# Two conditioning stages of a four-layer kernel computed inside differential attention, and its output transposes issued later

## The reference

```
silu(c) @ ada_w[i] + ada_b[i]  ->  shift, scale, gate       (layers 0 and 1: 3 x 1024 values, for c and c_ctx)
silu(c) @ w_ada + b_ada        ->  9 x 1024 values           (each of the two later layers, for c_2 and c_ctx_2)
h = rms_norm(x) * (1 + scale) + shift ;   x = x + gate * block(h)
```

```
q, k, v, g = h @ w_in ;  q, k = rope(rms_norm(q)), rope(rms_norm(k))     (keys and values also of the context)
attn = softmax(q1 k1) - lam * softmax(q2 k2) ;  o = attn @ v
y = (rms_norm(o) * silu(g)) @ w_out
```

## Time and profile before

| | |
|---|---|
| median of 3 runs (lowest to highest) | 5384.07 us (5380.6 to 5397.63) |
| the profiled execution's own time, and its span | 5410.06 us, 5408.3 us |
| PE busy | 4611.6 us, 85% of the span |
| PE weight load (beside PE) | 3517.2 us, 65% |
| DVE, ACT, POOL busy | 1674.7, 1243.5, 61.1 us |
| granted TensorE clock, mean | 0.914 |
| DMA | 331.41 MB, mean 61 GB/s |

### The profile page before, as it was taken

One profiled execution on the slowest core, in us unless ns is written; L12 is line 12 of the kernel. 1 busy time (PEld: TensorE's weight loads), 2 busy tenths in 40 slices (PEclk: granted clock), 3 DMA queues, 4 the chain that ended last, 5 costly groups with the idle time before them and its releaser, 6 DMA issues. The chain is left out here.

```text
span 5408.3 us, 86861 instructions
## 1 busy us (share of the span) xinstructions
PE 4611.6 (85%) x39756; PEld 3517.2 (65%) x39756; DVE 1674.7 (31%) x2184; ACT 1243.5 (23%) x1763; POOL 61.1 (1%) x65
## 2 busy tenths in 40 slices
PE   3789999997799975999977688999779997867998
PEld 2466666665466644888854356888658886534786
DVE  1345555552233321322222313222132222042433
ACT  1223333221144421311111203111031121021322
POOL 0000000000000000000002000000000000010000
PEclk7899999998899986999988778999879998978999
DMA  5100000001110018112111001121541211100222
GB/s 221 42 19 19 19 19 19 19 3 48 43 47 32 16 36 305 56 59 71 51 39 48 0 31 63 56 73 54 191 148 61 69 56 43 71 0 32 100 98 74
DMA packets 45308, 331.41 MB, mean 61 GB/s; under 512 B 4401, under 2 KB 8882, under 8 KB 21298
## 3 DMA queue, kind: packets, MB, share of 16 engines
q1 hardware_dynamic: 44978, 326.37, 16.8%
HBM read 324.26 MB, written 2.10 MB: 60 GB/s over the span
## 5 line engine op out<-in xcount | busy, mean ns | idle before, releaser
L617 PE MATMUL banks<-x_hi,w_hi 128*128 128x512 f32 (+1 forms) x2464 | 860.0, 349 | 29.6 <-DVE x_lo L718 29.6
L618 PE MATMUL banks<-x_lo,w_hi 128*128 128x512 f32 (+1 forms) x2464 | 855.7, 347 | 0.0
L619 PE MATMUL banks<-x_hi,w_lo 128*128 128x512 f32 (+1 forms) x2464 | 853.9, 347 | 0.0
L617 PEld LDWEIGHTS banks<-x_hi,w_hi 128*128 128x128 f32 x2464 | 471.0, 191 | 104.7 <-DVE x_lo L718 28.3
L619 PEld LDWEIGHTS banks<-x_hi,w_lo 128*128 128x128 f32 x2464 | 471.5, 191 | 57.4
L618 PEld LDWEIGHTS banks<-x_lo,w_hi 128*128 128x128 f32 x2464 | 472.2, 192 | 54.2
L618 PE MATMUL banks<-g_lo,w_hi 128*128 128x512 f32 (+1 forms) x1232 | 423.9, 344 | 0.0
L617 PE MATMUL banks<-g_hi,w_hi 128*128 128x512 f32 (+1 forms) x1232 | 423.6, 344 | 0.0
L619 PE MATMUL banks<-g_hi,w_lo 128*128 128x512 f32 (+1 forms) x1232 | 423.3, 344 | 0.0
L897 PE MATMUL banks<-x_normed_first,weight_ring_first 128*128 128x256 f32 (+1 forms) x1024 | 370.9, 503 | 3.0 <-ACT small L1219 3.0
L628 ACT CAST w_hi<-landing 128x2048 fp32r<-128x2048 f32 (+1 forms) x152 | 255.7, 1682 | 494.4 <-PE banks L619 494.4
(11 more groups left out here) (366 smaller groups left out, 5789.5 us busy)
## 6 DMA issues: line engine op xcount, KB each, us to landing
landing<-in_w SPq DMA_DIRECT2D x88, 1024.0 KB, 4.8
weight_ring_first<-in_ada_w SPq DMA_DIRECT2D x30, 2048.0 KB, 8.9
landing<-in_w SPq DMA_DIRECT2D x64, 704.0 KB, 4.0
weight_ring_end<-in_ada_w SPq DMA_DIRECT2D x18, 2048.0 KB, 8.8
weight_ring_first<-in_rw_pair SPq DMA_DIRECT2D x8, 2048.0 KB, 8.0
weight_ring_first<-in_da_head SPq DMA_DIRECT2D x8, 2048.0 KB, 7.8
weight_ring_mix<-in_w_in SPq DMA_DIRECT2D x12, 1024.0 KB, 4.8
weight_ring_mix<-in_w_out SPq DMA_DIRECT2D x8, 1024.0 KB, 4.9
```

The source lines that it names most:

```text
L617: nc.tensor.matmul(o, wh, xh[:, k, c0:c0 + cn], start=k == 0, stop=False)
L618: nc.tensor.matmul(o, wh, xl[:, k, c0:c0 + cn], start=False, stop=False)
L619: ins = nc.tensor.matmul(o, wl, xh[:, k, c0:c0 + cn], start=False, stop=k == kt - 1)
```

## The change

The second context load and the two later conditioning stages are gone as stages. Their 36 tiles of weights are loaded, multiplied, copied and transposed inside `diff_attention`, through one buffer of 2 MB in the arena. Four tiles stand in the part before the first scores, and one with each of the 4 x 8 blocks of queries, ahead of `values`; each tile's transpose stands ahead of the next block's `transposes`. The products and their transpose share the last quarter of bank 5. ACT does both copies out of PSUM; DVE adds all biases at once at the end. The values of both later layers have their own columns (48 to 191). The output transposes of head i-1, DVE's `finish` before them and ACT's copy after them now stand in head i, behind its first scores and 8 key products.

```diff
+                def ada_weights(n):
+                    if n:
+                        sp.wait_ge(rows_done.h, rows_done.at(n - 1, 4))
+                    sp.dma_start(ada_w, self.dram[f"ada2_w{n // 18}"][n % 18]).then_inc(ada_ready.h, 16)
...
+                head_weights(0)
+                sp.dma_start(lamv, self.dram["da_lam"]).then_inc(lam_loaded.h, 16)
+                sp.dma_start(rope, self.dram["tables"][:, at:at + n_rope]).then_inc(lam_loaded.h, 16)
+                ada_weights(0)
+                head_weights(1)
+                for n in range(1, EARLY):
+                    ada_weights(n)
+                sp.dma_start(self.x3(self.X)[:, :, LAT:T], self.dram["ctx2_t"]).then_inc(context_loaded.h, 16)
+                for i in range(HEADS):
+                    for q in range(QT):
+                        ada_weights(EARLY + QT * i + q)
+                        if q == 0 and i + 2 < HEADS:
+                            head_weights(i + 2)
...
+                    if i or q:
+                        ada_turn(EARLY + QT * i + q - 1)
                     for t in range(NB):
                         ins = nc.tensor.transpose(bank(4, T)[:, t * P:t * P + P], attn[:, q % 2, t * P:t * P + P], ident)
...
+                    ada_rows(EARLY + QT * i + q)
                     for t in range(NB):
                         ins = mm(bank(5)[:, 256:256 + P], AT[:, q % 2, t], V(i, t), start=t == 0, stop=t == NB - 1)
                     ins.then_inc(pv_done.h, 1)
...
+                def ada_rows(n):
+                    pe.wait_ge(ada_ready.h, ada_ready.at(n, 16))
+                    if n:
+                        pe.wait_ge(cols_taken.h, cols_taken.at(n - 1, 1))
+                    for kt in range(KT):
+                        for g in range(4):
+                            ins = mm(ada_bank[32 * g:32 * g + 32, :], sil[:, kt, :], ada_w[:, kt, g * P:g * P + P], start=kt == 0, stop=kt == KT - 1)
+                            if kt == KT - 1:
+                                ins.then_inc(rows_done.h, 1)
...
+                def ada_turn(n):
+                    pe.wait_ge(rows_copied.h, rows_copied.at(n, 1))
+                    nc.tensor.transpose(ada_bank, rows[:, n % 2], ident).then_inc(turned.h, 1)
...
                 fill = projections(0)
-                pull(fill, 20)
+                pull(fill, 10.2)
+                pe.wait_ge(silu_ready.h, silu_ready.at(0, 1))
+                ada_rows(0)
+                pull(fill, 6.8)
+                ada_turn(0)
+                ada_rows(1)
+                pull(fill, 3)
+                ada_turn(1)
                 pe.wait_ge(rec_ready.h, rec_ready.at(0, 1))
                 pe.wait_ge(lam_ready.h, lam_ready.at(0, 1))
                 broadcast(0, QT, 0)
                 broadcast(2, NB, 8)
+                ada_rows(2)
                 pull(fill, 8)
+                ada_turn(2)
                 rotate(0, 0, 1)
                 rotate(0, 1, 4)
+                ada_rows(3)
                 pull(fill, 99)
+                ada_turn(3)
...
                     scores(i, 0)
-                    pull(fill, 10.2)
+                    pull(fill, 6.8)
+                    if i:
+                        out_transposes(i - 1)
+                    pull(fill, 3.4)
                     scores(i, 1)
                     transposes(i, 0)
...
-                    out_transposes(i)
+                pe.wait_ge(pv_taken.h, pv_taken.at(HEADS - 1, QT))
+                ada_turn(ADA - 1)
+                out_transposes(HEADS - 1)
...
+                def take_rows(n):
+                    act.wait_ge(rows_done.h, rows_done.at(n, 4))
+                    if n >= 2:
+                        act.wait_ge(turned.h, turned.at(n - 2, 1))
+                    nc.scalar.copy(rows[:, n % 2], ada_bank).then_inc(rows_copied.h, 1)
+
+                def take_columns(n):
+                    act.wait_ge(turned.h, turned.at(n, 1))
+                    nc.scalar.copy(mods2[:, 4 * n:4 * n + 4], ada_bank.rearrange("p (j c) -> p j c", c=32)[:, :, 0:2]).then_inc(cols_taken.h, 1)
...
+                    if i or q:
+                        take_columns(EARLY + QT * i + q - 1)
                     nc.scalar.copy(AT[:, q % 2].rearrange("p t n -> p (t n)"), bank(4, T)).then_inc(at_ready.h, 1)
...
+                    take_rows(EARLY + QT * i + q)
                     r0 = stat[:, i % 2, q, 4:5]
                     nc.scalar.activation(O[:, q], bank(5)[:, 256:256 + P], ACT.Copy, scale=r0)
...
                     exps(i, 0)
+                    if i:
+                        take_out(i - 1)
                     if not last:
                         take_k(i + 1)
...
                         maxima(i, q, L)
+                        if q == 0 and i:
+                            finish(i - 1, L)
                         combine(i, q, L)
...
-                    finish(i, L)
+                finish(HEADS - 1, L)
+                dve.wait_ge(cols_taken.h, cols_taken.at(ADA - 1, 1))
+                L(tt(mods2, mods2, self.par("b_ada_2").unsqueeze(2).broadcast_to([P, 4 * ADA, 2]), ALU.add), ada_added)
...
-            K.load_context()
-            K.conditioning("ada2_w0", 72, 16, K.par("b_ada_2")[:, 0:72], mods[:, 0:72, :])
         for layer in range(DEPTH):
             last = layer == DEPTH - 1
             segs = LATENT if last else BOTH
-            m = lambda j: mods[:, 8 * j:8 * j + 8, :]
+            m = lambda j: mods[:, 48 + 72 * layer + 8 * j:48 + 72 * layer + 8 * j + 8, :]
```

More of the change, by code:

```diff
@@ L1481, in diff_attention @@
         QT, HEADS, QK_N = LAT // P, DA_HEADS, LAT + T
[L1482 to L1483 removed]
+        Yf, rope, QKf, raw, sq, VGf, Pf, attn, AT, O, On, junk, lams, ada_w, rows = self.carve(
+            self.arena, [8 * LAT, 2 * LAT, 2 * QK_N, QK_N, QK_N, 2 * 1280, 4 * T, 2 * T, 2 * T, LAT, LAT, P, 392, 4096, 2 * P])
         Y = Yf.rearrange("p (k n) -> p k n", n=LAT)
@@ L1503, in diff_attention @@
         bank = lambda b, n=512: PS[:, b * 512:b * 512 + n]
+        ada_w = ada_w.rearrange("p (k n) -> p k n", n=512)
+        rows = rows.rearrange("p (s n) -> p s n", n=P)
+        sil = small[:, 128:128 + 32 * KT].rearrange("p (k n) -> p k n", n=32)
+        mods2 = self.mods[:, 96:384].rearrange("p (t c) -> p t c", c=2)
+        ada_bank = bank(5)[:, 384:512]
+        EARLY, ADA = 4, 36
         half = lambda c: slice(HD * c, HD * c + HD)
@@ L1521, in _, with head_weights @@
             def _(sp):
-                for i in range(HEADS):
+                def head_weights(i):
                     if i >= 2:
@@ L1679, in take_vg @@
                     act.wait_ge(vg_done.h, vg_done.at(i, t + 1))
+                    if t == 0 and i >= 2:
+                        act.wait_ge(on_ready.h, on_ready.at(i - 2, 1))
                     n, o = (256, 256 * t) if t < QT else (P, 1024 + P * (t - QT))
@@ L1721, in take_out @@
                     nc.scalar.activation(Y[:, i], bank(4), ACT.Copy, scale=subln).then_inc(head_done.h, 1)
+                act.wait_ge(sil_zeroed.h, sil_zeroed.at(0, 1))
+                nc.scalar.activation(sil[:, :, 0:2], self.par("silu_in")[:, 16:32].rearrange("p (k c) -> p k c", c=2),
+                                     ACT.Silu).then_inc(silu_ready.h, 1)
                 act.wait_ge(lam_sums.h, lam_sums.at(0, 1))
@@ L1725, in _ @@
                 take_k(0)
+                take_rows(0)
                 take_q(0)
+                take_columns(0)
+                take_rows(1)
                 deviations(0)
-                for t in range(NB):
+                take_columns(1)
+                take_vg(0, 0)
+                take_rows(2)
+                take_vg(0, 1)
+                take_columns(2)
+                take_rows(3)
+                for t in range(2, NB):
                     take_vg(0, t)
+                take_columns(3)
                 gate(0)
@@ L1841, in diff_attention @@
                      pv_taken, ostd_ready, on_ready, ot_done, head_done)
-    def load_context(self):
-        nc, X3, loaded = self.nc, self.x3(self.X), self.sig("context_loaded", 16)
-        with nc.Block() as block:
-            @block.sync
-            def _(sp):
-                sp.dma_start(X3[:, :, LAT:T], self.dram["ctx2_t"]).then_inc(loaded.h, 16)
-                sp.wait_ge(loaded.h, loaded.at(0, 16))
-        self.advance(1, loaded)
     def mixers(self, layer, last):
@@ L2289, in build @@
                 return K.final_debug(K.X)
-            with ExitStack() as scope:
-                K.mixer_buffers(scope, f"end{layer}")
-                if not last:
-                    K.conditioning("ada2_w1", 72, 16, K.par("b_ada_2")[:, 72:144], mods[:, 0:72, :])
-                else:
-                    K.norm(LATENT, K.par("g_final"), None, None, K.x3(K.HN))
-                    K.final(K.x3(K.HN)[:, :, 0:LAT])
+        with ExitStack() as scope:
+            K.mixer_buffers(scope, "end")
+            K.norm(LATENT, K.par("g_final"), None, None, K.x3(K.HN))
+            K.final(K.x3(K.HN)[:, :, 0:LAT])
```

17 lines of the change are left out of this document (11 added, 6 removed).

## The result

| | before | changed | ratio |
|---|---|---|---|
| median, first comparison (4 runs of each) | 5390.85 us (5380.6 to 5404.43) | 5212.15 us (5204.89 to 5216.69) | 0.9656 [0.9641, 0.9671] |
| median, second comparison (9 and 5 runs) | 5407.38 us | 5213.15 us | 0.9645 [0.9632, 0.9658] |
| profiled execution, span | 5410.06, 5408.3 us | 5214.28, 5212.5 us | |
| PE, ACT busy; granted clock | 4611.6, 1243.5 us; 0.914 | 4547.7, 1240.9 us; 0.931 | |

What follows compares the result with a forecast made beforehand. PE sets the pace in seven full heads while loads bound the two stages: -242.3 + 15.9 + 7.0 + 20 = -199.4 us, so 5384.07 becomes 5184.7 us; range 5170 to 5202, wider 5168 to 5212.

Steps and rivals of the forecast that it cites:

- What bounds the kernel: In seven full heads PE sets the pace and DMA idles; both stages of modulation values are bound by loads.
- Removed: Both stages of modulation values go, replaced by direct steps of 0.26 and 0.5 us: gain 242.3 us.
- Added on PE, full heads: In heads 0 to 6, 28 tiles with transposes at 2.0 us each: +56.0 us, bounds 42 to 112.
- first rival: Each of 72 switches between 128- and 32-column operands costs PE 0.33 us: 23.8 us more, 5208.5 us; chance 0.12.
- Removed on PE, full heads: In seven heads output transposes no longer wait, -27.1 us, and the clock lost behind waits returns, -13.0 us.
- The single buffer: Tile loads with a round trip of 8.1 us fit the tightest distance of 9.3 us: no wait in full heads.
- second rival: Loads slower than alone, 12.8 us a transfer: some 10 us in each of seven heads, +85, 5270 us; chance 0.06.
- Before the first scores: Four tiles in the start of attention, waiting partly for weights: +7.0 us, bounds 5.2 and 23.
- The last head: Tiles wait for round trips of the single buffer: +15.0 at the higher clock, +21.4 at the lower, taken as +20 us.
- The third and fourth rivals: Third: moved output transposes still wait, +40, 5225 us, chance 0.07. Fourth: clock 1.2 GHz through attention, 5634 us, chance 0.01.
- three ranges: Last head from 15 to 22 us, start from 5 to 15, heads from 8 to 26, giving 5170 to 5202.

Runs made afterwards that it cites:

- kernel with wide sums: Kernel before with only the output transposes moved later, and each of the ten sums-of-squares products writing 48 columns instead of 2: 5368.17 us, 0.9919.
- three buffers: Changed kernel with the last head's second and third tiles loaded ahead into the idle head-weight buffers: 5204.66 us, 0.9623.

## Why the prediction was right

**What bounds the kernel** held: PE is busy in all of the seven heads and paid for what was put on it; an eighth of the loads changed nothing there, an eighth of the products did.

**Removed**: -242.5 against -242.3. The step assumed at 0.5 us measured 0.28. The two later layers kept their length, 1701.8 to 1699.1 us and 1439.4 to 1438.9. All other stages together moved by 0.75 us, and that is a balance: what stands ahead of attention, the same instructions, took 4.8 us longer in this profile.

**Added on PE, full heads**: the term that was mis-sized. 453.36 us less the 392.15 of the kernel without tiles, waits or falls is 61.2 us for 28 blocks, 2.19 each, where 2.0 were taken (1.88 for the tile and 0.12 for its transpose). The transpose was right: it takes 0.16 us, and the block's own transposes behind it are 0.05 shorter (1644.48 - 1643.82 = 0.66 against 1627.45 - 1626.74 = 0.71 before). The rows say where the other 0.2 is: the query products in front of a tile take 1651.44 - 1644.48 = 6.96 us, before 1634.32 - 1627.45 = 6.87 (the row between is 7.03 long, at 1627.45); the values behind it 1.54 instead of 1.43 (1654.86 - 1653.32, and 1635.75 - 1634.32). So 0.09 on the way in and 0.11 on the way out. This is the first rival's mechanism at 0.1 us a switch where the rival had 0.33: 5.6 us in 28 blocks by these rows, not 24 in 36. The measured 5212.15 us lies nearest to that rival's 5208.5 by number alone; most of the way there has another reason, told below. My argument against it, that no gap is seen on the way back, held only for the transpose of the stage; a values product behind a tile does show one. That the switch of operand shape is the cause is an inference from these neighbours, since no kernel made the same products without a switch. The Trainium skill, page "TensorEngine Tiling (Array Packing)", section Key Properties, has the drain at such a change without a price; the 0.09 and 0.11 us agree with it.

**Removed on PE, full heads**: -40.55 by the kernel with wide sums, -40.1 predicted. That the clock's 13 us would come back was right for the changed kernel and not for the same move alone, where another fall took 10.1 of them. The prediction knew only of falls behind waits; it was lucky that the changed kernel, in both profiles, had none of the others, for close relatives had three, four or six. The output transposes were ready 5.1 us after the next scores began (DVE's last scaling ended at 1633.63 + 1.14 = 1634.77, the scores began at 1629.72), and PE came at 8.5 (predicted at most 6.1 after the values ended, and 8.6).

**The single buffer**: no wait in seven heads, though the slowest of 36 loads took 13.1 us. The second rival is out, and the equal heads at 45 and 154 GB/s show it. In the last head it cost what the sum said: of the 17.4 to 17.8 us added, 13.5 go when three buffers are there. The Trainium skill's advice to double-buffer (page "Trainium Kernel Development and Optimization", Best Practices) was worth those 13.5 us, and nothing in the full heads.

**Before the first scores**: +7.5 against +7.0, with waits of 1.22 us ahead of tile 1, for ACT's copy of tile 0's values out of PSUM (an eighth of the loads left that wait as it was), and 2.35 for tile 2's weights. Tile 0 waited for nothing.

**The last head**: +17.8 against +20. The first tile starts 12.9 us into it (13 predicted), the next ones 10.2, 11.7 and 11.4 us apart (10.0 to 11.6). What was too high is the share of the lower clock: the first tile ran at the higher one, and so did the values behind the last tile (1.60 us, where 2.93 stood before).

**The third and fourth rivals** are out: no wait of the output transposes in seven heads, and a clock of 1.00 in the denser attention.

**From the profile to the median**: here most of the 27 us were lost. The sum missed by 3.6 us, and part of that is luck, since 5.2 us too little for the tiles stood against 2.2 too much for the last head. (The upper ends of its three ranges add up to 5204.8 us, not 5202; the measured median lies above both.) I then took it off the median of three runs, 5384.07, as if the 26 us between that and the profiled execution belonged to profiling. They don't: in later comparisons the median of the same kernel before was 5405.82, 5407.38 and 5403.61 us (9 runs each), beside the profiled 5410.06, and the second group of runs of the changed kernel had its lowest time in the profiled execution (5204.25, with a median of 5213.15). One place where executions differ can be seen: what stands ahead of attention, with the same instructions in all twelve profiles, took from 1425.5 to 1438.1 us. Medians of this kernel differ by 0.4% between groups of runs, and three runs don't fix the base. Between medians of one group the change was -178.7 and -194.2 us. From the base of the second group, 5407.38 - 199.4 = 5208.0, which is 5 us from its 5213.15.

## What to carry to other kernels

A stage bound by loads can be put into a stage bound by PE at the price of its PE work alone, if its loads fit between the places where their buffer is used; one buffer is enough where the gap from the end of one use to the start of the next is longer than issue and load take together (here at least 9.3 against 8.1 us), and not where it is shorter. The stretch after the overlap ends, here the last head, has to be costed apart and given its own buffers. Take a saving off a base only with the scatter of that base, and compare within one group of runs.

## What the runs showed of the hardware

- The granted clock can fall without any idle time of PE. Ten products of 2 columns (2.29 us for 20 passes) were followed by some 3.4 us at the lower level, 1.7 us lost each time: in six of seven heads of one kernel, in four of two others, in three of a fourth, and in none of the kernel before, the changed one (twice), the one with an eighth of the loads and the one with three buffers. With 48 columns the ten take 2.33 us and there was no fall in any of 21 heads (three kernels); in two of the three the 2-column form had falls in ten heads of 14. Which heads fall with the thin ones stays open: neighbours with the same instructions in the same order differ.
- A tile of 32 products of 128 x 32 by 128 x 128 costs 2.19 us with its transpose among 128-column products: 1.88 us from its start to the next instruction's, 0.11 for the transpose, and 0.2 at its neighbours before and behind it. One product more costs 0.055 us.
- The 36 tile loads of 2 MB landed in 7.8 to 13.1 us, and in the seven full heads, where PE was busy throughout, the traffic cost PE nothing: heads of 64.85 us at 154 and at 45 GB/s.
